# Another order of the weight tiles inside a group of a hybrid attention and pooling layer

## The chip, the cores and the metric

The kernel runs on one core of a Trainium2 chip. Its metric is the device time of one execution in microseconds. The engines are TensorE (PE, matrix products), VectorE (DVE), ScalarE (ACT), GpSimd (POOL) and SyncE (SP, which here only issues DMAs). Each works through its own list of instructions in order and waits for the others by semaphores.

## The reference

One layer takes 1024 frames of 2048 numbers, with 16 learned meta tokens ahead of them. Cut to what matters here:

```python
hn = _rmsnorm(h, norm_g)
pv, pg, q, k, v, ag = jnp.split(hn @ w_in, SPLITS, axis=-1)
# pooling: 4 channel groups, windows 2, 4, 8, 16
cg = jnp.cumsum(pv, axis=1)[..., group]
d = (cg - shifted_by_w(cg)) / cnt - pv[..., group]
pool_out = (d @ pool_w[group]) * pool_scale
# attention: 16 query heads, 2 key heads, window of two 64-frame chunks, meta tokens, a sink per head
attn_out = softmax_with_sink(q @ k.T / 8) @ v
h = h + concat([silu(pg) * pool_out, silu(ag) * attn_out]) @ w_out
```

## The kernel before, in words

The frames are worked on in two halves of 512. A half has 136 blocks of the input weights: 8 for keys and values, 32 for queries, and then four groups (g = 0 to 3) of 24 blocks. Four blocks in a row are one tile of 128 output channels, so a group has six tiles: two gates of attention (gates 0 and 1), the two tiles of pooling values, and two gates of pooling (gates 2 and 3). After both halves come 112 blocks of the output product.

To keep float32 accuracy on TensorE, each weight block is split into a high and a low part. SP loads a block into one of four raw buffers (line 400). ACT copies it to its high part `wh` (L616), VectorE subtracts for the low part `wl` (L964), and PE does three products for each of four slices, twelve matmuls to a block (L1435, L1436, L1442). ACT and VectorE split block s + 3 while PE works on block s. "Place s" of their lists means that split with all the work that the lists `todo` and `ahead` put beside it. ACT's split in place s waits until PE has finished block s - 1.

Beside the tiles each group runs the attention of four units of two heads (u = 0 to 3), written out by place. PE does the scores of a unit after blocks a and a + 1, its transposes after block a + 5 and its value products after block a + 7, where a is 2, 7, 11, 15 in group 0 and 0, 5, 10, 15 in groups 1 to 3. Between them lie, on VectorE, the sums of the scores (L1154), the row maximum (L1158, L1162) in place a + 2, and the normalising (L1168 to L1179) in place a + 4; on ACT the exponentials (L844, L847) in place a + 3. In place a + 6 ACT copies the transposed parts and VectorE takes their low parts (`pt`, `pm`), and in place a + 8 ACT (`o_low`) and VectorE (`o_out`, L1198 to L1206) take the unit's output. `qs` are the high and low parts of the queries for the next unit.

A gate's tile is read from its bank by VectorE (`gate_in`, L1212), ACT takes the tanh (L870) and VectorE closes it (`gate_out`, L1216). All four gates share one buffer for the tanh. Pooling values are copied out by ACT (`pv_out`, in front of the split of its place), in the first half from two banks, since 16 columns of earlier frames or meta tokens belong to them. POOL scales a tile (L578; in the first half after a small product, L573) and adds it up in g + 1 steps (L586), each of which doubles the window. Then VectorE subtracts (`pooled`, L1221), ACT and VectorE make the high and low parts of d (`d_high`, `d_low`), and at the end of the group PE multiplies d by `pool_w` (L1675 to L1677) and VectorE multiplies by gate and scale (`mix_out`, L1131). After each chain of sums POOL also issues two 1 MB DMAs that build sums of output weights (`weight_sums`). In the first half SP also stores finished tiles and loads frames of the next half (`spill`, `next_frames`) behind the loads of blocks 6 and 14.

The tiles share three PSUM banks R0 to R2. Before a tile PE waits until its bank has been read (`gate_bank_read`, `s_pve`). In the first half the second pooling tile starts on its first bank and waits for its second one, which the first pooling tile filled, in the middle of its first block (`second_free`).

Of the kernel before, what the change touches and what calls it, by code (L numbers as in the profile page):

```python
# [51 lines left out]
ROWT = HALF // P  # L52
UNITS = 4

FIRST_SPLITS = ({3: (1, 2), 7: (3, 4), 11: (5, 6), 15: (7,)},
# [35 lines left out]
def hymba_layer(nc, xcat, norm_g, w_in, w_out, pool_w, vecs, consts, out):  # L91
# [6 lines left out]
    with ctx:  # L98
# [130 lines left out]
        KB, VB = ((R[0], R[1]), (PM,)), ((R[2], O), (R[0],))  # L229
        PVB = (((R[2], R[0]), (R[1], R[2])), ((R[2],), (R[1],)))  # L230

# [139 lines left out]
        def product_done(eng, h, n):  # L371

            eng.wait_ge(s_blk, ONE + h * IN_BLKS + n + TILE_BLKS)
# [21 lines left out]
        def _(sp):  # L395
# [44 lines left out]
            for h in range(HALVES):  # L440
                h0 = h * IN_BLKS
                for n in range(RAW if h == 0 else 0, KV_BLKS):
                    if h and n == KV_BLKS - 1:
                        spill(GROUPS - 1)
                    load_block(h0 + n, n % RAW, w_in[TILE_BLKS * (n % 2) + n // 2, :, :])
                if h:
                    next_frames(GROUPS - 1)
                with sp.Fori(0, PAIRS) as j:
                    for b in range(TILE_BLKS):
                        n = KV_BLKS + j * TILE_BLKS + b  # L450
                        load_block(h0 + n, b % RAW, w_in[n, :, :])

                def group(g):
                    sp.wait_ge(s_pwl, ONE + h * GROUPS + g)
                    sp.dma_start(pw_raw.rearrange("p (a c) -> p a c", a=2),
                                 pool_w[g, :, :].rearrange("(a p) c -> p a c", p=P)).then_inc(s_pw, 16)
                    for b in range(G_BLKS):
                        n = KV_BLKS + Q_BLKS + g * G_BLKS + b
                        load_block(h0 + n, b % RAW, w_in[n, :, :])
                        if h == 0 and g and b == 6:  # L460
                            spill(g - 1)
                        if h == 0 and g and b == 14:
                            next_frames(g - 1)

                if h == 0:
                    for g in range(GROUPS):
                        group(g)
                else:
                    with sp.Fori(0, GROUPS) as g:
                        group(g)  # L470
# [143 lines left out]
        def _(act):  # L614
# [51 lines left out]
            for h in range(HALVES):  # L666
# [168 lines left out]
                def group(g):  # L835
# [36 lines left out]
                    def pv_out(jj):  # L872
                        product_done(act, h, n0 + 8 + 4 * jj)
                        act.wait_ge(s_dl, ONE + G * 2)
# [30 lines left out]
                    todo[4].append((gate_tanh, 0, R[0]))  # L905
                    todo[8].append((gate_tanh, 1, R[1]))
                    todo[16].append((d_high, 0))
                    todo[20].append((gate_tanh, 2, R[0]))
                    todo[21].append((d_high, 1))
                    todo[24].append((gate_tanh, 3, R[1]))  # L910
# [13 lines left out]
                    for s in range(G_BLKS + 1):  # L924
                        if s == 12:
                            pv_out(0)
                        elif s == 16:
                            pv_out(1)
# [33 lines left out]
        def _(dve):  # L962
# [27 lines left out]
            for h in range(HALVES):  # L990
# [145 lines left out]
                def group(g):  # L1136
# [73 lines left out]
                    def gate_in(n, bank):  # L1210
                        product_done(dve, h, n0 + (0, 4, 16, 20)[n])
                        nc.vector.tensor_tensor(gate[n], bank[:, :], rb[:, META:COLS], ALU.mult).then_inc(s_gv[n], 1)  # L1212
# [45 lines left out]
                    todo[5].append((gate_out, 0))  # L1258
                    todo[8].append((gate_in, 1, R[1]))
                    todo[9 if g else 14].append((gate_out, 1))  # L1260
                    todo[15].append((pooled, 0))
                    todo[18].append((d_low, 0))
                    todo[20].append((pooled, 1))
                    todo[22].append((d_low, 1))
                    todo[20].append((gate_in, 2, R[0]))
# [153 lines left out]
        def _(pe):  # L1419
# [89 lines left out]
            for h in range(HALVES):  # L1509
# [9 lines left out]
                def gate_bank_read(n, count):  # L1519
                    pe.wait_ge(s_gv[n], ONE + count)  # L1520
# [59 lines left out]
                def group(g, e, late):  # L1580
# [62 lines left out]
                    def events(s):  # L1643
                        for f, *a in when.get(s, ()):
# [9 lines left out]
                    gate_bank_read(3, G)  # L1654
                    tile(h, n0 + 4, (R[1],), own, events=events, slot0=4)
                    gate_bank_read(0, G + 1)
                    pe.wait_ge(s_pve, ONE + G * 2)
                    pe.wait_ge(s_me, ONE + G * 2)
                    tile(h, n0 + 8, PVB[h][0], pv_spans(h, g), events=events, slot0=8)
                    gate_bank_read(1, G + 1)  # L1660
                    tile(h, n0 + 12, PVB[h][1], pv_spans(h, g), events=events, slot0=12,
                         second_free=2 * G + 1 if h == 0 else 0)
                    pe.wait_ge(s_pve, ONE + G * 2 + 1)
                    tile(h, n0 + 16, (R[0],), own, events=events, slot0=16)
                    pe.wait_ge(s_pve, ONE + G * 2 + 2)
                    tile(h, n0 + 20, (R[1],), own, events=events, slot0=20)
# [119 lines left out]
```

## Time and profile before

| | |
|---|---|
| time, median of 3 runs | 1179.48 us (1178.87 to 1179.82) |
| the profiled execution | 1178.72 us, of which the span is 1176.6 us |
| busy, share of the span | PE 1166.1 us (99%), weight load 991.8 (84%), VectorE 889.7 (76%), ACT 616.1 (52%), POOL 115.5 (10%) |
| chain that ended last | PE 99% |
| costliest lines outside PE | L964 (low parts) 283.4 us, L616 (high parts) 240.8 us, L1084 (reciprocals) 53.6 us, L844 (exponentials) 51.2 us |
| POOL's sums | L586 50.3 us in 40 operations of 1257 ns, L578 20.9 us in 16 |
| DMA | 171.26 MB, mean 146 GB/s |

The span goes from the first to the last instruction that the profiler shows; the time also has what lies around it. "Busy" is the union of an engine's instructions, so that overlapping matmuls count once.

### The profile page before, as it was taken

The page shows a single profiled execution, that of the slowest core. Times are in us where ns is not written, and L with a number is a line of the kernel's source. Part 1 is how long each engine was busy: PE and PEld are TensorE (multiplying, and loading weights), DVE is VectorE, ACT ScalarE, POOL GpSimd, SP SyncE. Part 2 cuts the span into 40 slices and gives each one's busy share as a digit, 9 for nine tenths or more (in the row PEclk, how much of TensorE's full clock was granted, in tenths as well). Part 3 has the DMA queues.
Part 4 walks back from the last instruction along what each step waited for, and adds up shares of the span by engine and source line. Part 5 has one row for each costly group of instructions (what it writes and reads, how often), then busy time and mean ns, then how long its engine had stood idle before and what let it go on. Part 6 is the DMA issues. An engine that isn't in the chain of part 4 may idle for free.

```text
span 1176.6 us, 17280 instructions
## 1 busy us (share of the span) xinstructions
PE 1166.1 (99%) x5882; PEld 991.8 (84%) x5882; DVE 889.7 (76%) x1545; ACT 616.1 (52%) x1400; POOL 115.5 (10%) x133
## 2 busy tenths in 40 slices
PE   7999999999999999999999999999999999999998
PEld 7888898898898988888888888888888888888887
DVE  4678778787786885678788786987977977656676
ACT  5743366554665655643565655655544544444442
POOL 0000011020040220000011030220400000100001
PEclk9999999999999999999999999999999999999999
DMA  7354339455486333445357372392346544553443
GB/s 242 92 162 156 95 99 218 132 189 184 132 177 179 118 90 108 134 138 171 94 129 179 92 242 76 97 226 81 88 137 223 167 136 134 185 176 123 142 145 134
DMA packets 85486, 171.26 MB, mean 146 GB/s; under 512 B 8464, under 2 KB 11792, under 8 KB 85264
## 3 DMA queue, kind: packets, MB, share of 16 engines
q1 hardware_dynamic: 72000, 129.08, 35.3%
q0 software_dynamic: 13120, 40.90, 14.1%
q8 instruction: 44, 0.72, 0.3%
q14 instruction: 34, 0.28, 0.1%
q10 hardware_dynamic: 288, 0.28, 0.1%
HBM read 157.64 MB, written 46.14 MB: 173 GB/s over the span
## 4 chain that ended last, share of the span: by engine, by line
PE 99%; DMA 0%; DVE 0%; ACT 0%; issue 0%; SPq 0%; DVEq 0%; ACTq 0%
PE R L1435 18%; PE R L1436 18%; PE R L1442 18%; PE R L1725 3%; PE R L1723 3%; PE R L1724 3%; PE OP L1725 2%; PE S L1725 2%; PE OP L1723 2%; PE S L1723 2%; PE OP L1724 2%; PE S L1724 2%; PE S L1593 1%; PE OP L1617 1%; PE OP L1442 1%; PE OP L1435 1%
## 5 line engine op out<-in xcount | busy, mean ns | idle before, releaser
L964 DVE TENSOR_TENSOR wl<-raw,wh 128x512 fp32r<-128x512 f32 x384 | 283.4, 740 | 192.9 <-ACT wh L616 190.6
L616 ACT ACTIVATE wh<-raw 128x512 fp32r<-128x512 f32 x384 | 240.8, 629 | 351.0 <-PE OP L1725 165.9
L1435 PE MATMUL R<-act_h,wh 128*128 128x512 f32 (+5 forms) x1056 | 380.6, 365 | 0.0
L1436 PE MATMUL R<-act_l,wh 128*128 128x512 f32 (+5 forms) x1056 | 378.5, 364 | 0.0
L1442 PE MATMUL R<-act_h,wl 128*128 128x512 f32 (+5 forms) x1048 | 362.2, 365 | 0.0
L1436 PEld LDWEIGHTS R<-act_l,wh 128*128 128x128 f32 x1056 | 198.6, 188 | 28.6
L1435 PEld LDWEIGHTS R<-act_h,wh 128*128 128x128 f32 x1056 | 198.3, 188 | 28.7
L1442 PEld LDWEIGHTS R<-act_h,wl 128*128 128x128 f32 x1048 | 188.3, 188 | 32.1
L1725 PE MATMUL R<-wh,mix_l 128*128 128x512 f32 x168 | 65.4, 389 | 0.0
L1723 PE MATMUL R<-wh,mix_h 128*128 128x512 f32 x168 | 65.4, 389 | 0.0
L1724 PE MATMUL R<-wl,mix_h 128*128 128x512 f32 x168 | 65.4, 389 | 0.0
L870 ACT ACTIVATE row_buf<-scr 128x512 f32<-128x512 f32 x32 | 20.2, 632 | 79.5 <-DVE scr L1212 79.5
L1154 DVE TENSOR_REDUCE scr<-S 128x288 f32<-128x576 f32 x56 | 42.3, 756 | 25.3 <-PE S L1593 24.5
L1084 DVE RECIPROCAL scr<-scr 128x512 f32<-128x512 f32 x16 | 53.6, 3347 | 0.0
L844 ACT ACTIVATE scr<-scr,nmax 128x144 f32<-128x144 f32 x128 | 51.2, 403 | 3.4 <-DVE nmax L1162 3.3
L586 POOL TENSOR_TENSOR scr<-scr 128x513 f32<-128x513 f32 (+6 forms) x40 | 50.3, 1257 | 3.1
L578 POOL TENSOR_TENSOR scr<-scr,row_buf 128x512 f32<-128x512 f32 (+4 forms) x16 | 20.9, 1306 | 268.3 <-ACT scr L616 257.9
L1725 PE MATMUL OP<-wh,mix_l 128*128 128x512 f32 x112 | 43.6, 389 | 0.0
L1724 PE MATMUL OP<-wl,mix_h 128*128 128x512 f32 x112 | 43.6, 389 | 0.0
L1723 PE MATMUL S<-wh,mix_h 128*128 128x512 f32 x112 | 43.6, 389 | 0.0
L1724 PE MATMUL S<-wl,mix_h 128*128 128x512 f32 x112 | 43.6, 389 | 0.0
L1725 PE MATMUL S<-wh,mix_l 128*128 128x512 f32 x112 | 43.6, 389 | 0.0
(252 smaller groups left out, 1957.8 us busy)
## 6 DMA issues: line engine op xcount, KB each, us to landing
raw<-w_in_blocks SPq DMA_DIRECT2D x271, 256.0 KB, 2.7
wsum<-w_out_in POOLq DMA_DIRECT2D x24, 1024.0 KB, 12.1
raw<-wsum SPq DMA_DIRECT2D x64, 256.0 KB, 2.6
raw<-w_out_in SPq DMA_DIRECT2D x48, 256.0 KB, 3.3
c<-xcat SPq DMA_DIRECT2D x32, 256.0 KB, 3.5
out<-c POOLq DMA_DIRECT2D x28, 256.0 KB, 2.9
mixed<-xcat SPq DMA_DIRECT2D x10, 512.0 KB, 5.2
mx<-mixed SPq DMA_DIRECT2D x8, 512.0 KB, 3.5
```

The lines of the kernel that those rows point to most:

```text
L586: ins = pool.tensor_tensor(dst[:, lo:COLS], src[:, lo:COLS], src[:, lo - step:COLS - step], ALU.add)
L616: return nc.scalar.activation(dst, src, ACT.Copy)
L844: nc.scalar.activation(prob[:, c, :], prob[:, c, :], ACT.Exp, bias=nmax[:, c:c + 1], accum_out=den[:, c:c + 1]).then_inc(s_ex, 1)
L964: return nc.vector.tensor_tensor(dst, a, b, ALU.subtract)
L1084: nc.vector.reciprocal(q_rs[t % 2], q_rs[t % 2]).then_inc(s_qrs, 1)
L1154: nc.vector.tensor_reduce(to, both, AX.X, ALU.add).then_inc(s_sm, 1)
L1435: mm(o, wh[:, b, w], xh, start=(k == 0), stop=False)
L1436: mm(o, wh[:, b, w], xl, start=False, stop=False)
L1442: last = mm(o, wl[:, b, w], xh, start=False, stop=(k == KT - 1))
L1723: mm(banks[r], mh, wh[:, slot, :], start=(k == 0), stop=False)
L1724: mm(banks[r], mh, wl[:, slot, :], start=False, stop=False)
L1725: last = mm(banks[r], ml, wh[:, slot, :], start=False, stop=(k == HK - 1))
```

## The change

The blocks of a group come in another order: gate 0, the two pooling tiles, gate 1, gates 2 and 3. SP takes the addresses of the blocks from a table, the layout in memory stays as it was. ACT's copies of the pooling tiles, VectorE's subtraction and both parts of d are put four places sooner, so that POOL's sums follow four blocks sooner, and gate 1's read, tanh and closing product eight places later (the closing product from place 9, in group 0 from 14, to 17). The banks of the two pooling tiles and PE's waits for them are exchanged to match.

```diff
--- before.py
+++ after.py
@@ -51,6 +51,9 @@
 IN_BLKS = KV_BLKS + Q_BLKS + GROUPS * G_BLKS
 ROWT = HALF // P
 UNITS = 4
+
+GROUP_TILES = (0, 2, 3, 1, 4, 5)
+GATE_BLK = (0, 12, 16, 20)
 
 FIRST_SPLITS = ({3: (1, 2), 7: (3, 4), 11: (5, 6), 15: (7,)},
                 {3: (3,), 7: (4,), 11: (5, 6), 15: (7,)})
@@ -227,7 +230,7 @@
         OP = ctx.enter_context(nc.psum_tensor("OP", [P, 2, BLK], f32))
         O, PM = OP[:, 0, :], OP[:, 1, :]
         KB, VB = ((R[0], R[1]), (PM,)), ((R[2], O), (R[0],))
-        PVB = (((R[2], R[0]), (R[1], R[2])), ((R[2],), (R[1],)))
+        PVB = (((R[2], R[1]), (R[0], R[2])), ((R[2],), (R[0],)))
 
         OV = OP[:, :, :].rearrange("p b (c s n) -> p (b c) s n", c=2, s=2)
         QB = [S[:, 0, :]] + [(R[1][:, :], R[0][:, :], O)[t % 3] for t in range(PAIRS - 1)]
@@ -455,8 +458,9 @@
                     sp.dma_start(pw_raw.rearrange("p (a c) -> p a c", a=2),
                                  pool_w[g, :, :].rearrange("(a p) c -> p a c", p=P)).then_inc(s_pw, 16)
                     for b in range(G_BLKS):
-                        n = KV_BLKS + Q_BLKS + g * G_BLKS + b
-                        load_block(h0 + n, b % RAW, w_in[n, :, :])
+                        n = KV_BLKS + Q_BLKS + g * G_BLKS
+                        load_block(h0 + n + b, b % RAW,
+                                   w_in[n + GROUP_TILES[b // TILE_BLKS] * TILE_BLKS + b % TILE_BLKS, :, :])
                         if h == 0 and g and b == 6:
                             spill(g - 1)
                         if h == 0 and g and b == 14:
@@ -870,7 +874,7 @@
                         nc.scalar.activation(gate_t, gate[n], ACT.Tanh, scale=0.5).then_inc(s_ge[n], 1)
 
                     def pv_out(jj):
-                        product_done(act, h, n0 + 8 + 4 * jj)
+                        product_done(act, h, n0 + 4 + 4 * jj)
                         act.wait_ge(s_dl, ONE + G * 2)
                         for n, (bank, c) in enumerate(zip(PVB[h][jj], pv_spans(h, g))):
                             ins = copy(pv[jj][:, c], bank[:, 0:c.stop - c.start])
@@ -903,10 +907,10 @@
                         todo[22].append((qdiag, 0, g + 1))
                     todo[2].append((pw_high,))
                     todo[4].append((gate_tanh, 0, R[0]))
-                    todo[8].append((gate_tanh, 1, R[1]))
-                    todo[16].append((d_high, 0))
+                    todo[16].append((gate_tanh, 1, R[1]))
+                    todo[12].append((d_high, 0))
                     todo[20].append((gate_tanh, 2, R[0]))
-                    todo[21].append((d_high, 1))
+                    todo[17].append((d_high, 1))
                     todo[24].append((gate_tanh, 3, R[1]))
                     if isinstance(g, int) and g == 2:
                         todo[2].append((v_operand, 1))
@@ -922,9 +926,9 @@
                             for n, s in enumerate((21, 22, 24)):
                                 todo[s].append((mix_high, n))
                     for s in range(G_BLKS + 1):
-                        if s == 12:
+                        if s == 8:
                             pv_out(0)
-                        elif s == 16:
+                        elif s == 12:
                             pv_out(1)
                         if s == 1 and isinstance(g, int) and g == 0:
                             q_sqrt(PAIRS - 1)
@@ -1208,7 +1212,7 @@
                                                        ALU.mult, ALU.mult).then_inc(s_oe, 1)
 
                     def gate_in(n, bank):
-                        product_done(dve, h, n0 + (0, 4, 16, 20)[n])
+                        product_done(dve, h, n0 + GATE_BLK[n])
                         nc.vector.tensor_tensor(gate[n], bank[:, :], rb[:, META:COLS], ALU.mult).then_inc(s_gv[n], 1)
 
                     def gate_out(n):
@@ -1256,12 +1260,12 @@
                     todo[6].insert(0, (pw_low,))
                     todo[4].append((gate_in, 0, R[0]))
                     todo[5].append((gate_out, 0))
-                    todo[8].append((gate_in, 1, R[1]))
-                    todo[9 if g else 14].append((gate_out, 1))
-                    todo[15].append((pooled, 0))
-                    todo[18].append((d_low, 0))
-                    todo[20].append((pooled, 1))
-                    todo[22].append((d_low, 1))
+                    todo[16].append((gate_in, 1, R[1]))
+                    todo[17].append((gate_out, 1))
+                    todo[11].append((pooled, 0))
+                    todo[14].append((d_low, 0))
+                    todo[16].append((pooled, 1))
+                    todo[18].append((d_low, 1))
                     todo[20].append((gate_in, 2, R[0]))
                     todo[21].append((gate_out, 2))
                     todo[24].append((gate_in, 3, R[1]))
@@ -1652,17 +1656,17 @@
                     tile(h, n0, (R[0],), own, events=events, slot0=0)
                     pe.wait_ge(s_qn, h * PAIRS + 8)
                     gate_bank_read(3, G)
-                    tile(h, n0 + 4, (R[1],), own, events=events, slot0=4)
-                    gate_bank_read(0, G + 1)
                     pe.wait_ge(s_pve, ONE + G * 2)
                     pe.wait_ge(s_me, ONE + G * 2)
-                    tile(h, n0 + 8, PVB[h][0], pv_spans(h, g), events=events, slot0=8)
-                    gate_bank_read(1, G + 1)
-                    tile(h, n0 + 12, PVB[h][1], pv_spans(h, g), events=events, slot0=12,
+                    tile(h, n0 + 4, PVB[h][0], pv_spans(h, g), events=events, slot0=4)
+                    gate_bank_read(0, G + 1)
+                    tile(h, n0 + 8, PVB[h][1], pv_spans(h, g), events=events, slot0=8,
                          second_free=2 * G + 1 if h == 0 else 0)
                     pe.wait_ge(s_pve, ONE + G * 2 + 1)
+                    tile(h, n0 + 12, (R[1],), own, events=events, slot0=12)
+                    pe.wait_ge(s_pve, ONE + G * 2 + 2)
                     tile(h, n0 + 16, (R[0],), own, events=events, slot0=16)
-                    pe.wait_ge(s_pve, ONE + G * 2 + 2)
+                    gate_bank_read(1, G + 1)
                     tile(h, n0 + 20, (R[1],), own, events=events, slot0=20)
 
                     pe.wait_ge(s_dl, ONE + G * 2 + 2)
```

## Rows read from the trace of the kernel before

**Rows 1.** Waits, TensorE alone: total us, times, longest.

```profile
PE R L1453 <- DMA scr<-xcat: 5.7, 1, 5.7
```

**Rows 2.** Busy us (operations): PE, PEld, DVE, ACT, POOL; clock; DMA share; GB/s.

```profile
130.00:865.00 735.00, 734.83 (x3856) 630.27 (x3855) 580.05 (x1081) 417.88 (x1046) 95.65 (x92) 1.00 0.50 138
```

**Rows 3.** Timeline (start, length), PE, second half, group 1, end of block 10.

```profile
673.76 0.39 PE L1442 MATMUL R<-act_h,wl 128*128 128x512 f32 x1
674.00 0.60 PE L1605 MATMUL PT<-cst,scr 128*128 128x128 f32 x4
```

**Rows 4.** Timeline, VectorE, second half, group 1, places 8 and 9.

```profile
666.73 0.68 DVE L1198 TENSOR_TENSOR o_part<-OP,o_part 64x512 f32<-64x512 f32 x1
...
668.34 0.42 DVE L1206 SCALAR_TENSOR_TENSOR mixed<-scr 128x256 f32<-128x256 f32 x1
668.68 0.68 DVE L1212 TENSOR_TENSOR scr<-R,row_buf 128x512 f32<-128x512 f32 x1
670.59 0.69 DVE L964 TENSOR_TENSOR wl<-raw,wh 128x512 fp32r<-128x512 f32 x1 [1.22 <-ACT wh L616]
671.31 0.85 DVE L964 TENSOR_TENSOR qs<-mixed,qs 64x256 fp32r<-64x256 f32 x2
...
673.28 0.22 DVE L1179 TENSOR_TENSOR pnm<-scr,rden 128x64 f32<-128x64 f32 x1
```

**Rows 5.** Timeline, PE, second half, group 0, end of block 20.

```profile
629.37 0.62 PE L1605 MATMUL PT<-cst,scr 128*128 128x128 f32 x4
```

**Rows 6.** Timeline, VectorE, second half, group 0, places 16 to 19.

```profile
617.10 1.41 DVE L964 TENSOR_TENSOR wl<-raw,wh 128x512 fp32r<-128x512 f32 x1
...
620.58 1.18 DVE L964 TENSOR_TENSOR pm<-OP,pm 16x128 fp32r<-16x128 f32 x4
...
625.29 0.69 DVE L964 TENSOR_TENSOR wl<-raw,wh 128x512 fp32r<-128x512 f32 x1 [1.29 <-ACT wh L616]
...
629.06 0.22 DVE L1179 TENSOR_TENSOR pnm<-scr,rden 128x64 f32<-128x64 f32 x1
```

**Rows 7.** Timeline, ACT, second half, group 1, place 8.

```profile
665.35 0.63 ACT L616 ACTIVATE wh<-raw 128x512 fp32r<-128x512 f32 x1 [1.19 <-PE R L1442]
...
668.09 0.28 ACT L847 ACTIVATE esink<-nmax,vec 128x4 f32<-128x4 f32 x1
```

**Rows 8.** Operations with the tile raw: its loads, issue to landing.

```profile
DMA to landing us min/median/max: 2.4/2.7/10.2
```

**Rows 9.** Timeline, ACT, second half, group 3, place 12.

```profile
828.82 0.60 ACT L616 ACTIVATE scr<-R 128x512 f32<-128x512 f32 x1 [0.57 <-PE R L1442]
829.31 0.21 ACT L616 ACTIVATE scr<-pv_last 128x16 f32<-128x16 f32 x1
829.42 0.62 ACT L616 ACTIVATE wh<-raw 128x512 fp32r<-128x512 f32 x1
```

**Rows 10.** Timeline, POOL, second half, group 3, first chain.

```profile
829.60 1.29 POOL L578 TENSOR_TENSOR scr<-scr,row_buf 128x512 f32<-128x512 f32 x1 [56.60 <-ACT scr L616]
830.97 1.40 POOL L586 TENSOR_TENSOR scr<-scr 128x527 f32<-128x527 f32 x1
832.45 1.06 POOL L586 TENSOR_TENSOR scr<-scr 128x525 f32<-128x525 f32 x1
...
835.05 1.30 POOL L586 TENSOR_TENSOR scr<-scr 128x513 f32<-128x513 f32 x1
```

**Rows 11.** Timeline, VectorE, second half, group 3, beside that chain.

```profile
830.07 1.37 DVE L964 TENSOR_TENSOR wl<-raw,wh 128x512 fp32r<-128x512 f32 x1
...
835.59 1.05 DVE L1206 SCALAR_TENSOR_TENSOR mixed<-scr 128x256 f32<-128x256 f32 x1
```

**Rows 12.** Timeline, ACT, first half, group 3, place 8.

```profile
389.43 0.63 ACT L616 ACTIVATE wh<-raw 128x512 fp32r<-128x512 f32 x1 [1.16 <-PE R L1442]
```

**Rows 13.** Timeline, PE, first half, group 3, end of block 10.

```profile
398.63 0.60 PE L1605 MATMUL PT<-cst,scr 128*128 128x128 f32 x4
```

**Rows 14.** Timeline, ACT, second half, group 0, place 17.

```profile
618.19 1.13 ACT L616 ACTIVATE pm<-OP 16x128 fp32r<-16x128 f32 x4
```

## The prediction

> **What bounds the kernel now.** I read the waits of TensorE first, since an engine at 99% of the span is the bound unless it hides stops. Its longest wait by far is 5.7 us for the first load [rows 1], before anything that the change edits. The busy table of one long stretch, from shortly before the first group to the end of the last (130 to 865 us), has 734.83 us of PE in 735.00, at a granted clock of 1.00 [rows 2]. Inside the groups no idle time is left to win. A later, earlier or cheaper operation on another engine is worth nothing there; only a new stop of PE can move the time. So the question is how much slack stands in front of each thing that PE waits for, and I went from the waits to the timelines to measure it.
>
> Matmuls of one tile start 0.23 to 0.24 us apart [rows 3], 12 to a block, so a block takes 2.7 us at least and four blocks 11 us or more. In groups 1 to 3 PE's nearest appointment is the transposes of unit 1, which come at the end of block 10. In group 1 of the second half they start at 674.00 [rows 3], and the softmax pieces that they read were ready at 673.50 (673.28 + 0.22) [rows 4]: half a microsecond of slack. In group 0 the transposes of unit 3 (end of block 20) start at 629.37 [rows 5], their operand being ready at 629.28 (629.06 + 0.22) [rows 6]: 0.09 us, which is no slack but the time of the signal. Everything else that I measured (the low parts before the value products, the scores, the split weights) has more than a microsecond.
>
> **The change, part by part.** The same 24 blocks, matmuls, copies and loads are there before and after, so PE's sum of work is the same. A two-bank block (first half of the sequence) only stands at another place. SP issues the same 24 loads in another order from another address: 0. The banks: gate 1, which had R1 from block 4 to place 8, now has it from block 12 to place 16, and each tile that takes a bank still finds four blocks of 2.7 us between the read of it and its own start, as before. The second bank of pooling tile 1 is still given free by ACT's first copy at the start of the same block, and at that moment (place 8) ACT is idle and waiting for PE: its split there had waited 1.19 us for PE [rows 7], so the copy starts as promptly as it did at place 12. The wait for the previous group's mixing results moves from before block 8 to before block 4, but still has blocks 0 to 3, 11 us, in front of it. All that: 0. The wait for the last low parts of d before the mixing products is met four places sooner, where PE did not stop: 0.
>
> POOL's chain. It now runs in places 8 to 10 and 12 to 14 in place of 12 to 14 and 16 to 18. Its accumulating DMAs are issued four blocks sooner, one pair after the other at the same distance from each other. Between the last pair of the Q stage (issued at block 28) and the first group's (now behind block 48) some 20 blocks are left, over 50 us. The pair can now meet the loads of the next half's frames, which SP issues at place 8. Loads of a raw block land after 2.4 to 10.2 us [rows 8], and are issued about four blocks, 11 us, before ACT splits them, with three more blocks until PE wants them: 0.
>
> What costs is that ACT and VectorE get new work between the scores of unit 1 and its transposes. Laid onto the times of group 1 of the second half (block 7 ends just before 665.35):
>
> 1. ACT does the copies of pooling tile 0 first. Where they now stand, the split follows 0.60 us after the copy's start (829.42 against 828.82) [rows 9]. So the split at 665.35 [rows 7] comes at 665.95, is done at 666.58, and the exponentials, which ended at 668.37, end at 668.97.
> 2. In return gate 1's read (0.68 us) and its closing product (about as long) leave VectorE's places 8 and 9, and the tanh between them leaves ACT. They mattered: VectorE stood 1.22 us waiting for ACT's next split, which was behind that tanh [rows 4]. Without POOL's chain VectorE would take its low part of the weights at 669.7, and the softmax pieces would be ready near 672.6, sooner than now.
> 3. POOL's chain starts 0.78 us after ACT's copy (829.60 against 828.82) [rows 9, 10]: here at 666.1. And it holds VectorE up: a wl of 0.69 us takes 1.37 when it starts in a POOL operation, and ends 0.55 us after that operation (831.44 against 830.89) [rows 10, 11]. The POOL operation that comes next then ends 0.93 after the wl (832.37) [rows 10]. The 256-wide product of L1206, 0.42 us alone [rows 4], took 1.05 and ended 0.29 after POOL (836.64 against 836.35) [rows 10, 11]. Reductions and operations with a PSUM operand are not held up.
>
> The Trainium skill, "SBUF — State Buffer", section "SBUF: two separate sides", says the same of the cause: a VectorE operation with two SBUF inputs and a GpSimd operation that reads SBUF take one pair of ports by an exclusive lock, whoever starts first, for the whole instruction. The trace agrees with the waiting. By that rule a POOL operation that already waits would go before VectorE's next one, and the change would cost the 1.45 us of the alternating case below; by a VectorE that passes the ports on to itself it would cost nothing.
>
> Group 3 has five POOL operations. Op 1: 666.1 to 667.4. The wl of 666.58 ends at 667.95. Op 2 ends 668.9. The two kinds of o_out operations that read PSUM take 1.61 us (666.73 to 668.34) [rows 4], to 669.56. Op 3 (1.06 us [rows 10]) runs 668.95 to 670.0, so L1206 ends at 670.3. Now the trace of before has no row for what comes next: VectorE's next operations (wl, the two qs, the divisions) all have two SBUF inputs, and POOL waits for its turn. **If they alternate**, op 4 ends 671.2, wl 671.75, op 5 672.7, the first qs 672.95. From the end of the first qs (671.73) to the pieces' end (673.50) it is 1.77 [rows 4], so they are ready at 674.7, and with the 0.09 of the signal PE starts at 674.8 instead of 674.0: 0.8 us lost. **If VectorE keeps the ports**, wl ends 670.9, the pieces are ready at 673.1, and nothing is lost; POOL's chain ends some 2 us later, and has until place 11, which is after 677. In the first half's group 3 PE comes to the transposes 9.20 us after ACT's split of place 8 (398.63 against 389.43) [rows 12, 13] and not 8.65 (674.00 against 665.35) [rows 3, 7], and POOL has one small product more, 0.3 us by its place ahead of the chain: 0.8 - 0.55 + 0.3 = 0.55 lost. Group 2 has four POOL operations: the first qs starts at 671.8, the pieces are ready at 674.0, 0.1 lost in the second half and none in the first. Group 1, three operations: ready before 673.3, none. Sum if they alternate: 0.8 + 0.55 + 0.1 = 1.45 us; bound below: 0.
>
> Group 0, where there is no slack. From place 14 to 19 VectorE has five of the moved operations (low d 0, gate 1, pooled 1, closing product, low d 1) where it had three (closing product, pooled 0, low d 0): 2 x 0.68 = 1.36 us more before the normalising of unit 3. What covers it: POOL's second chain is gone from place 16, so that the wl at 617.10 takes 0.69 and not 1.41 [rows 6]; and in place 18 VectorE has 1.29 us in which it waits for ACT [rows 6], where two of the five (closing product and low d 1) fit. ACT is held by its tanh until gate 1 is read, near 617.8, so its small copies (618.19 to 619.32 [rows 14]) end 1.2 us later, at about 620.55, and VectorE takes the low parts from them at 620.6, when it does now (620.58) [rows 6]. The row maximum and all behind it stay in their place within 0.1 us. I take 0 to 0.1 for each half; bound above: 1.36 each, 2.7 us together, if no cover holds.
>
> **The sum.** The profiled run took 1178.72 us, 2.12 more than its span of 1176.6, and the median of the three runs 1179.48, 0.76 above it. 1178.72 + 1.45 = 1180.2, with group 0's 0 to 0.1 left at 0; against the median 1180.9. The bounds put together: 0 below, 1.45 + 2.7 = 4.15 above.
>
> **Rivals.** *POOL and VectorE do not alternate, or the loss is otherwise swallowed.* For it: the work taken from places 8 and 9 is larger than the work put there. Time: 1179.5. *VectorE falls behind in group 0.* For it: a slack of 0.09 us and five operations for three, with ACT held behind a tanh; against it, the two covers. With nothing covered, 1179.48 + 4.15 = 1183.6, slower; it decides from 0.9 us for each half on (with the 1.45, over 2.36). *DMAs collide*: POOL's megabyte sums beside the frames' loads. A raw load would have to land over 15 us after its issue to stop PE (seven blocks of 2.7, less the splits); the worst landed after 10.2 [rows 8]. Under 1 in 50. *Faster*: PE would have to have a wait in the groups that the new order removes. All that [rows 2] leaves is 0.17 us, and the time would be 1179.3, no change either.
>
> **Chances.** Alternating, 1180.9 or so: 0.40. Nothing lost, 1179.5: 0.36. Group 0 behind, by part or all of its 2.7, to 1183.6: 0.19; some of this stays under the bound. Something that I don't see, to either side: 0.05. I count a difference of over 0.2% (2.36 us) as change, about what a measurement of this kernel tells from none. Faster 0.04, same 0.78, slower 0.18. My value is that of the alternating case, 1180.9; the range goes from 1178.6 (the case of no loss, less the 0.9 us that runs of before differ by) to 1183.6. The likeliest case alone is 1180 to 1181.5.
>
> **What would show it.** In the trace after: no idle time of PE in blocks 4 to 11, and none at the second bank in block 8; the split of place 8 on ACT 0.6 us later; the wl of places 8 and 9 stretched by POOL and those of 16 and 17 not; a wait of PE for L1179 before the transposes of unit 1 in group 3, under a microsecond, none in group 1; the transposes of unit 3 in group 0 within 0.1 us of the end of block 20's matmuls. I am wrong if PE waits in group 0 for over half a microsecond, or in group 1 at all, or if the sum of PE's busy time changes by more than its waits.

## The result, and the profile after

The changed kernel takes 1181.88 us (median of 20 runs, 1180.71 to 1183.9), the kernel before 1179.8 us beside it (20 runs, 1178.87 to 1181.77). The ratio is 1.0017, with a 95% interval of 1.001 to 1.0024: slower by 2.1 us, and clear of noise, though the middle of the interval lies under the 0.2% that I had taken as a bound. I had forecast 1180.9, from three runs of the kernel before whose median was 1179.48; the twenty have 0.32 us more.

The waits of TensorE in the changed kernel (total us, times, longest; before, [rows 1] had the first of them as the longest, and the last two were there too):

```profile
PE R L1457 <- DMA scr<-xcat: 5.3, 1, 5.3
PE PT L1609 <- DVE pnm L1183: 1.6, 2, 1.0
PE R L1499 <- DVE act_l L980: 1.0, 1, 1.0
PE OP L1499 <- DVE act_l L980: 0.2, 1, 0.2
```

One line is new: twice the transposes wait for the softmax pieces of VectorE. (Lines after the diff are four higher, so L1609 is what L1605 was, and L968, L1183, L1210 and L590 are L964, L1179, L1206 and L586.) The busy table of the stretch with the groups, which in [rows 2] left PE 0.17 us idle, now leaves 1.80:

```profile
130.00:867.00 737.00, 735.20 (x3855) 629.82 (x3854) 579.75 (x1082) 420.53 (x1046) 97.17 (x92) 1.00 0.50 138
```

The larger of the two waits is in group 3 of the second half. On ACT, whose split of place 8 would have come at 817.35 or so, the copies of pooling tile 0 are first, and the split comes 0.74 us after their start:

```profile
817.30 0.60 ACT L620 ACTIVATE scr<-R 128x512 f32<-128x512 f32 x1 [1.10 <-PE R L1446]
817.91 0.22 ACT L620 ACTIVATE scr<-pv_last 128x16 f32<-128x16 f32 x1
818.04 0.62 ACT L620 ACTIVATE wh<-raw 128x512 fp32r<-128x512 f32 x1
```

POOL's chain beside it (operations 1 to 3; 4 and 5 as one row, 822.19 to 825.02):

```profile
818.21 1.30 POOL L582 TENSOR_TENSOR scr<-scr,row_buf 128x512 f32<-128x512 f32 x1 [55.11 <-ACT scr L620]
819.58 1.39 POOL L590 TENSOR_TENSOR scr<-scr 128x527 f32<-128x527 f32 x1
821.05 1.06 POOL L590 TENSOR_TENSOR scr<-scr 128x525 f32<-128x525 f32 x1
...
822.19 2.83 POOL L590 TENSOR_TENSOR scr<-scr 128x521 f32<-128x521 f32 x2
```

VectorE in the same stretch:

```profile
818.69 1.36 DVE L968 TENSOR_TENSOR wl<-raw,wh 128x512 fp32r<-128x512 f32 x1 [0.63 <-ACT wh L620]
819.97 0.67 DVE L1202 TENSOR_TENSOR o_part<-OP,o_part 64x512 f32<-64x512 f32 x1
820.68 0.87 DVE L1206 TENSOR_TENSOR scr<-OP,o_part 64x256 f32<-64x256 f32 x2
821.58 0.82 DVE L1210 SCALAR_TENSOR_TENSOR mixed<-scr 128x256 f32<-128x256 f32 x1
822.32 1.54 DVE L968 TENSOR_TENSOR wl<-raw,wh 128x512 fp32r<-128x512 f32 x1
823.89 1.85 DVE L968 TENSOR_TENSOR qs<-mixed,qs 64x256 fp32r<-64x256 f32 x2
...
826.86 0.22 DVE L1183 TENSOR_TENSOR pnm<-scr,rden 128x64 f32<-128x64 f32 x1
```

As long as POOL's chain runs, each operation with two operands in SBUF is stretched: the low part of the weights twice (0.69 alone), L1210 from 0.42 to 0.82, the pair of `qs` from 0.85 [rows 4] to 1.85 (all of it in the first of the two). L1202, which reads the PSUM bank OP, runs inside POOL's second operation and takes its usual 0.67. The second wl starts at 822.32, 0.13 us after POOL's fourth operation has been issued, and ends at 823.86. PE then stands still for 0.96 us:

```profile
825.78 0.39 PE L1446 MATMUL R<-act_h,wl 128*128 128x512 f32 x1
827.13 0.66 PE L1609 MATMUL PT<-cst,scr 128*128 128x128 f32 x4 [0.96 <-DVE pnm L1183]
```

Without the wait the transposes would have started 0.23 to 0.24 us after the matmul, as in [rows 3], at 826.02. So 1.11 us are lost. Group by group, from the end of a group's start block to the end of its last one (worked out from the matmuls that close the blocks), against the kernel before:

| us over before | group 0 | group 1 | group 2 | group 3 |
|---|---|---|---|---|
| first half | +0.24 | -0.12 | -0.07 | +0.79 |
| second half | +0.19 | -0.02 | +0.09 | +1.13 |

The eight sum to 2.23. With the start of the run, 0.09 us shorter, and rounding they are the 2.13 us by which the last matmul comes later, and the span grew by 2.1 (1176.6 to 1178.7). Behind the groups nothing moved: the output stage has the same length to 0.01 us.

### The profile page after: what moved, and what is told of

Same layout as the page of the kernel before. It is cut to its first block, busy times and chain, and to the rows that moved or that the text cites. A ratio compares the mean times of both kernels' runs of the same rounds, so it can differ in the third digit from the quotient of the medians.

```text
span 1178.7 us, 17282 instructions
## 1 busy us (share of the span) xinstructions
PE 1167.0 (99%) x5882; PEld 992.1 (84%) x5882; DVE 889.2 (75%) x1545; ACT 618.9 (53%) x1400; POOL 117.0 (10%) x133
## 4 chain that ended last, share of the span: by engine, by line
PE 97%; DVE 2%; DMA 0%; issue 0%; ACT 0%; SPq 0%; ACTq 0%; DVEq 0%
PE R L1439 18%; PE R L1440 18%; PE R L1446 18%; PE R L1727 3%; PE R L1729 3%; PE R L1728 3%; PE S L1727 2%; PE OP L1727 2%; PE OP L1729 2%; PE S L1729 2%; PE OP L1728 2%; PE S L1728 2%; PE S L1597 1%; PE PT L1609 1%; PE OP L1446 1%; PE OP L1440 1%
## 5 line engine op out<-in xcount | busy, mean ns | idle before, releaser
L968 DVE TENSOR_TENSOR wl<-raw,wh 128x512 fp32r<-128x512 f32 x384 | 281.1, 734 | 192.1 <-ACT wh L620 191.2
L590 POOL TENSOR_TENSOR scr<-scr 128x513 f32<-128x513 f32 (+6 forms) x40 | 51.7, 1293 | 3.1
L1727 PE MATMUL OP<-wh,mix_h 128*128 128x512 f32 x112 | 43.6, 389 | 0.0
```

Of the source, the lines that this page charges most:

```text
L590: ins = pool.tensor_tensor(dst[:, lo:COLS], src[:, lo:COLS], src[:, lo - step:COLS - step], ALU.add)
L968: return nc.vector.tensor_tensor(dst, a, b, ALU.subtract)
L1727: mm(banks[r], mh, wh[:, slot, :], start=(k == 0), stop=False)
```

## The experiments

Each was timed beside the kernel before on the same chip. The groups' sums are against the profiled kernel before, as in the table above; each is one execution, but they leave out the stages ahead of the groups, whose end moved by up to 1.0 us from run to run.

| run | median us | before | ratio (95%) | groups, first half | groups, second half |
|---|---|---|---|---|---|
| changed kernel | 1181.88 | 1179.8 | 1.0017 (1.001 to 1.0024) | 0.24, -0.12, -0.07, 0.79 | 0.19, -0.02, 0.09, 1.13 |
| sums late | 1182.86 | 1179.77 | 1.0025 (1.0015 to 1.0035) | 2.29, -0.12, -0.07, -0.09 | 1.95, -0.02, 0.00, -0.01 |
| short chain | 1179.13 | 1179.77 | 0.9993 (0.9984 to 1.0002) | 0.22, -0.12, -0.07, -0.09 | 0.25, 0.00, 0.09, -0.01 |
| five operations | 1184.73 | 1179.77 | 1.0041 (1.0028 to 1.0055) | 0.59, 0.51, 0.54, 0.75 | 0.37, 0.81, 0.87, 1.16 |
| queries behind | 1180.8 | 1179.77 | 1.0012 (1.0003 to 1.0021) | 0.20, -0.14, -0.07, 0.25 | 0.25, 0.00, 0.00, 0.73 |
| tanh later | 1181.17 | 1179.87 | 1.0007 (0.9998 to 1.0016) | 0.02, -0.12, -0.07, 0.76 | 0.03, 0.00, 0.07, 1.14 |
| copy behind | 1185.85 | 1179.87 | 1.0049 (1.0036 to 1.0063) | 0.23, -0.12, -0.07, 0.78 | 0.25, 0.81, 1.55, 4.16 |
| both repairs | 1180.92 | 1179.87 | 1.0009 (1.0 to 1.0018) | 0.02, -0.12, -0.07, 0.25 | 0.03, 0.00, 0.00, 0.72 |
| queries ahead | 1179.88 | 1179.73 | 0.9999 (0.999 to 1.0008) | -0.01, -0.12, -0.07, -0.06 | 0.04, 0.00, 0.00, 0.74 |

My theory after the result: POOL and VectorE take turns at operations with two SBUF operands, and in group 3 the chain is long enough to hold up VectorE until PE waits. The rival: ACT's copy, now ahead of the exponentials, delays them by 0.6 us, and VectorE only follows.

### Sums late: the new order with POOL at its old places

```diff
                         pool.wait_ge(s_pve, ONE + (h * GROUPS + g) * 2 + jj + 1)
+                        pool.wait_ge(s_blk, ONE + h * IN_BLKS + KV_BLKS + Q_BLKS + g * G_BLKS + 12 + 4 * jj)
...
-                    todo[12].append((d_high, 0))
+                    todo[16].append((d_high, 0))
-                    todo[17].append((d_high, 1))
+                    todo[21].append((d_high, 1))
...
-                    todo[11].append((pooled, 0))
-                    todo[14].append((d_low, 0))
-                    todo[16].append((pooled, 1))
-                    todo[18].append((d_low, 1))
+                    todo[15].append((pooled, 0))
+                    todo[18].append((d_low, 0))
+                    todo[20].append((pooled, 1))
+                    todo[22].append((d_low, 1))
```

> The new order of blocks and of gate 1, but POOL's sums start four blocks later, where they stood before, and the subtraction and both parts of d go back to their places (15 to 22). Theory (ports shared by POOL and VectorE make the waits): PE's wait before the transposes of unit 1 in group 3 (0.96 and 0.62 us) and the 0.1 us of group 2 are gone. In group 0 the cover that I counted on is gone too: VectorE has gate 1's two operations beside POOL's chain in places 16 and 17, so that the wait before the transposes of unit 3, 0.2 us now, should grow to between 0.7 and 1.5 us in each half. Time within 1 us of the changed kernel. Rival (ACT's copy ahead of the exponentials makes them): the waits of group 3 stay at 0.6 us or more.

The waits of groups 2 and 3 are gone (group 3 is at -0.01 and -0.09), with ACT's copy still ahead of the exponentials. The rival as the whole cause is out. The time is 0.98 us over the changed kernel, just inside what I had written. What I did not see is a part of the other side: group 0 grew by 2.29 and 1.95 us. The wait before the transposes, 1.1 us, is in the range of 0.7 to 1.5, but there were two waits, not one. The first waits of TensorE in that kernel:

```profile
PE PT L1610 <- DVE pnm L1184: 2.1, 2, 1.1
PE OP L1622 <- ACT pm L621: 0.8, 1, 0.8
PE OP L1622 <- issue: 0.4, 1, 0.4
```

ACT's tanh of gate 1 waits for VectorE, which waits for POOL; behind the tanh on ACT stand unit 2's small copies, and PE's value products of unit 2 wait for those, a wait that I had not priced (in the second half ACT stands for 4.32 us before that tanh). Each half loses about 2 us, which my rival on group 0 had bounded at 1.36, and moving POOL's chain forward avoids it: the new order of blocks needs the sooner sums.

### Short chain: three POOL operations in group 3

```diff
-                        for lev in range(g + 1):
+                        last = min(g, 1) if g == 3 else g
+                        for lev in range(last + 1):
...
-                            if lev < g:
+                            if lev < last:
```

> The changed kernel, with POOL's chain in group 3 cut from five operations to three (it leaves out the last two doublings, so group 3's pooling is that of a window of 4). Theory (ports): group 3 behaves as group 1, PE's wait before the transposes of unit 1 there is gone in both halves, time 1.8 to 2.1 us under the changed kernel. Rival (ACT's copy): waits of 0.6 us or more stay, time within 0.7 us of the changed kernel.

Group 3 is as long as before to 0.1 us in both halves, and no wait of PE for the pieces is left in the trace. ACT's copy stands where it stood. The median fell by more than I had written (2.75 us, 1181.88 to 1179.13, not timed side by side, against 1.8 to 2.1) and more than the groups account for (2.0).

### Five operations in every group

```diff
                         src = pv[jj]
+                        for _ in range(GROUPS - 1 - g):
+                            if chained:
+                                pool.wait_ge(s_add, chained)
+                            pool.tensor_tensor(psum_w[1][:, first + 1:COLS], src[:, first + 1:COLS],
+                                               src[:, first:COLS - 1], ALU.add).then_inc(s_add, 1)
+                            chained += 1
```

> The changed kernel, with additional POOL additions (their results are overwritten) so that each group's chain has five operations, as group 3's. Theory (ports): groups 1 and 2 now lose what group 3 loses, 1.0 to 1.2 us each in the second half and 0.6 to 0.9 each in the first, so 3.2 to 4.2 us over the changed kernel, less the 0.1 that group 2 loses now; group 0 adds 0 to 1 us, since its unit 2 meets a longer second chain with 1.1 us of slack. Rival (ACT's copy): no change, within 0.7 us of the changed kernel.

The loss follows the number of POOL operations:

```profile
PE PT L1615 <- DVE pnm L1189: 4.1, 7, 1.0
```

Groups 1 and 2 go from about 0 to 0.5 in the first half and to 0.81 and 0.87 in the second, group 0 adds 0.35 and 0.18. Over the changed kernel the eight groups have 3.37 us more (5.60 against 2.23), inside what I had written, with each second-half group some 0.15 under its part; by the medians, not timed side by side, it is 2.85 (1184.73 against 1181.88), under it. Without additional ACT work the waits came into groups that had none.

### Queries behind the normalising

```diff
-                        if u < UNITS - 1 and at[u + 1] - 1 == at[u] + 4:
+                        behind = g > 0 and u == 1
+                        if not behind and u < UNITS - 1 and at[u + 1] - 1 == at[u] + 4:
                             todo[at[u] + 4].append((qdiag, u + 1, g))
...
                             todo[at[u] + 4].append((normalise, u))
+                        if behind:
+                            todo[at[u] + 4].append((qdiag, u + 1, g))
```

> The changed kernel, with VectorE's two low parts of the queries for unit 2 (groups 1 to 3) behind unit 1's normalising in place 9 and not ahead of it. Theory (VectorE's queue, held by POOL, sets the pieces): the first operation of the normalising meets POOL's fifth operation instead, but 0.85 us of queue are gone, so the wait in group 3 falls from 0.96 to 0.0 to 0.3 us in the second half and to 0 in the first, time 1.5 to 2.0 us under the changed kernel. The scores of unit 2, which wait for the moved parts, have over 3 us of slack and lose at most 1.5. Rival (the exponentials, late by ACT's copy, set the pieces): nothing changes, since the normalising waits for them.

The wait before the transposes shrank as expected, from 1.1 us to 0.2, but a new one took part of its place. PE in group 3 of the second half:

```profile
825.74 0.39 PE L1449 MATMUL R<-act_h,wl 128*128 128x512 f32 x1
826.19 0.66 PE L1612 MATMUL PT<-cst,scr 128*128 128x128 f32 x4
...
827.16 0.53 PE L1600 MATMUL S<-band,qs 128*128 128x288 f32 x2 [0.20 <-DVE qs L968]
```

and VectorE:

```profile
823.73 1.27 DVE L1172 TENSOR_TENSOR dtot<-den,esink 128x4 f32<-128x4 f32 x1
...
826.17 0.86 DVE L968 TENSOR_TENSOR qs<-mixed,qs 64x256 fp32r<-64x256 f32 x2
```

The scores of unit 2 come in the same pause of PE as unit 1's transposes, and the queries' low parts, which had over 3 us of slack, now have none. The group saved 0.4 us in the second half and 0.54 in the first, not 1.1 and 0.9, and the median is 1.1 us under the changed kernel, where I had written 1.5 to 2.0. The first of the rows on VectorE is instructive by itself: a sum over four columns, 0.16 us alone, takes 1.27: it has two SBUF operands, and POOL's fifth operation, which ends 0.02 us before it, is in front of it. (A rival by which ACT's exponentials set the pieces is out here too: they would have been as late.)

### Group 0's tanh later

```diff
-                    todo[16].append((gate_tanh, 1, R[1]))
+                    if g:
+                        todo[16].append((gate_tanh, 1, R[1]))
...
                     todo[17].append((d_high, 1))
+                    if not g:
+                        todo[17].append((gate_tanh, 1, R[1]))
```

> The changed kernel, with gate 1's tanh in group 0 behind unit 2's small copies and the high part of d on ACT (place 17) and not ahead of them (place 16). Theory (in group 0 ACT is held behind the tanh until VectorE has read gate 1, and the row maximum follows late): the small copies start some 1.5 us earlier, and the 0.2 us before the transposes of unit 3 are gone in each half; at most 0.4 us in all, too little for the times, so the blocks and the wait decide. Rival (VectorE has too many operations in places 16 to 18): the 0.2 us stay.

Group 0's 0.24 and 0.19 fall to 0.02 and 0.03. The cause was ACT held behind the tanh, not the number of VectorE's operations.

### ACT's copy behind the exponentials, second half only

```diff
-                        if s == 8:
+                        if s == 8 and h == 0:
                             pv_out(0)
...
                         for f, *a in todo[s]:
                             f(*a)
+                        if s == 8 and h:
+                            pv_out(0)
```

> The changed kernel; in the second half alone ACT's copy of pooling tile 0 stands behind the exponentials of place 8 and not ahead of the split, so that the exponentials come 0.6 us sooner and POOL's first chain starts some 3 us later. Theory (ports): the chain now lies on VectorE's queries' low parts and on the normalising itself, which all have two operands in SBUF, so PE waits before the transposes of unit 1 also in groups 1 and 2 of the second half, and in group 3 no less than 0.8 us; time 0.5 to 3 us over the changed kernel. Rival (ACT's copy ahead of the exponentials): the wait of group 3 in the second half falls by 0.6 us, and groups 1 and 2 have none.

This was the sharpest test, since theory and rival say opposite signs, and it went the way of the ports: in the profiled execution groups 1 to 3 of the second half lost 0.81, 1.55 and 4.16 us, though their exponentials came sooner. The first half, which was not edited, is as in the changed kernel. VectorE in group 3, second half:

```profile
825.13 1.36 DVE L970 TENSOR_TENSOR wl<-raw,wh 128x512 fp32r<-128x512 f32 x1 [0.89 <-ACT wh L620]
826.52 2.38 DVE L970 TENSOR_TENSOR qs<-mixed,qs 64x256 fp32r<-64x256 f32 x2
828.93 0.90 DVE L1174 TENSOR_TENSOR dtot<-den,esink 128x4 f32<-128x4 f32 x1
829.87 0.18 DVE L1176 RECIPROCAL rden<-dtot 128x4 f32<-128x4 f32 x1
830.08 1.38 DVE L1181 TENSOR_TENSOR scr<-scr,rden 128x256 f32<-128x256 f32 x1
```

and POOL (operations 3 and 4 as one row):

```profile
824.66 1.28 POOL L582 TENSOR_TENSOR scr<-scr,row_buf 128x512 f32<-128x512 f32 x1 [58.16 <-ACT scr L620]
826.02 1.39 POOL L590 TENSOR_TENSOR scr<-scr 128x527 f32<-128x527 f32 x1
827.49 2.32 POOL L590 TENSOR_TENSOR scr<-scr 128x525 f32<-128x525 f32 x2
829.89 1.28 POOL L590 TENSOR_TENSOR scr<-scr 128x513 f32<-128x513 f32 x1
```

Five POOL operations, five stretched ones on VectorE (the wl, both `qs`, dtot and the first product behind the reciprocal), in strict turn; only the reciprocal, with one operand, takes its usual 0.18. By the medians the run is 4.0 us over the changed kernel, more than the 3 that I had given as the most, and the profiled execution, one of the longest of the five, has 5.4 more in its groups. A second reason for that, in this execution, is told in the last section.

### Both repairs, and the queries ahead

"Both repairs" is the two edits above (queries behind, tanh later) in one kernel.

> The changed kernel with both repairs: the queries' low parts behind unit 1's normalising, and in group 0 gate 1's tanh behind the small copies. Theory: PE's waits in the groups fall under 0.3 us in sum, and the time comes to within 0.5 us of the kernel before, on either side: PE was busy throughout in it, so nothing beyond that can be had. Rival (the new order costs PE something besides its waits): 0.7 us or more over the kernel before with no wait in the trace.

The rest of group 3 stays (0.72 and 0.25), group 0 is repaired; the sum of the groups is 0.83 us over before, so over the 0.3 that I had written. The median is 1.05 us over before, outside the 0.5 too. There is no loss outside the waits of group 3, which speaks against this run's rival. The last kernel has the tanh later and puts the queries' low parts ahead instead, into the 0.6 us in which VectorE waits for ACT's split:

```diff
-                        if u < UNITS - 1 and at[u + 1] - 1 == at[u] + 4:
+                        if g and u == 1:
+                            ahead[8].append((qdiag, u + 1, g))
+                        elif u < UNITS - 1 and at[u + 1] - 1 == at[u] + 4:
                             todo[at[u] + 4].append((qdiag, u + 1, g))
```

> The changed kernel with gate 1's tanh in group 0 behind the small copies, and in groups 1 to 3 the two low parts of the queries for unit 2 at the head of VectorE's place 8, ahead of the low part of the weights, where VectorE waits for ACT's copy and split anyway. Theory (in group 3 it is the operations with two SBUF operands behind POOL's third operation that are each held up): the queue behind POOL's fourth operation is then the low part of the weights and the normalising alone, so the wait in group 3 falls from 0.96 and 0.62 us to under 0.4 in the second half and 0 in the first, with no new wait before the scores of unit 2; the blocks of the groups sum to within 0.4 us of the kernel before, the time to 0.7 us. Rival (each operation moved out only makes the one behind it wait as long): 0.6 us or more stay in group 3 of the second half.

1179.88 us against 1179.73, ratio 0.9999 (0.999 to 1.0008): by the medians the loss of the change is undone. The first half is shorter than before in all four groups, by 0.26 us in all, and its wait in group 3 is gone. Group 3 of the second half keeps one wait of 0.5 us and 0.74 of length, over the 0.4 that I had written, so the eight groups sum to 0.52 over before and not to 0.4 at most. The rival, which wanted 0.6 or more there, fits that one group and not the first half:

```profile
817.64 1.86 DVE L971 TENSOR_TENSOR qs<-mixed,qs 64x256 fp32r<-64x256 f32 x2
819.54 1.44 DVE L971 TENSOR_TENSOR wl<-raw,wh 128x512 fp32r<-128x512 f32 x1
...
823.24 1.80 DVE L971 TENSOR_TENSOR wl<-raw,wh 128x512 fp32r<-128x512 f32 x1
```

The second of the two `qs` began 0.28 us behind POOL's first operation (818.08 against 817.80) and took 1.43 us, and the low part of place 9, the last row, had POOL's fifth operation (823.11 to 824.49) in front of it. No kernel beat the one before by more than its interval.

## Why the prediction was right

**PE is the bound and only a new stop can move the time.** Right: the loss is made of waits of PE, and with most of them removed the median is that of before. Only the reading of [rows 2] was too strict: the busy time hides short stops between matmuls, so that the new order could win 0.28 us in the first half (below), where the table left 0.17 in all.

**Where it would stop.** Right in groups 1 to 3: transposes of unit 1 in group 3 (both halves), 0.1 us in group 2 of the second half, nothing in group 1. The signs that I named for them came too: the split of place 8 later by 0.7 us, the wl of places 8 and 9 stretched, those of 16 and 17 in group 0 at 0.68. The chance of "no loss" because VectorE keeps the ports (0.36) fell: the two alternate. Against POOL's fourth operation, which was issued at 822.19 while L1210 held the ports until 822.40 (821.58 + 0.82), the wl at 822.32 had to wait. In the kernel with the copy behind, it is so five times in a row. The Trainium skill, "SBUF — State Buffer", section "SBUF: two separate sides", has whoever starts first hold the pair for its whole instruction; these rows agree, and show what follows from it for two queues that both always have a next operation: turn by turn.

**Its size.** This is what was off, though the time stayed in the range; it passed the 1180 to 1181.5 that I had given for the likeliest case alone. Of the 0.95 us between 1180.93 and 1181.88, 0.32 are the median of the kernel before, and the rest are the terms. The term for group 3 of the second half was 0.8 and measured 1.1. By its own steps: first qs done at 7.7 us after block 7 by my sum, at 8.0 in the trace (825.32 against 817.27, the end of the block). POOL's fourth operation ended where I had it (5.95 by the sum, 6.0 in the trace). The fifth and last one ended 1.17 us after the wl (825.02 against 823.86) and not 0.93. That last one was 0.24 us longer than the rule I had taken from one of the middle ones; my rows had a last operation [rows 10] that met no such wl. The remaining 0.1 was there from the start of the chain: POOL's first operation came 0.94 us after the end of the block (818.21 against 817.27), where my sum has 0.85, and each operation behind it is set by that. ACT's split did come 0.74 us after the copy and not 0.60, but that moved nothing, as the wl had to wait for POOL's first operation anyhow. The term for the first half was 0.55 and measured 0.88 (0.79 in the changed kernel against -0.09 with the short chain); its fifth operation too ended 1.17 us after the wl.

**Group 0.** I took 0 to 0.1 in each half, and it was 0.24 and 0.19; the sign that I named, transposes within 0.1 us of the end of block 20's matmuls, did not come. The covers held to 0.2 us. Of the chain, ACT's small copies were late by that much: VectorE's low parts waited for them,

```profile
621.53 1.19 DVE L968 TENSOR_TENSOR pm<-OP,pm 16x128 fp32r<-16x128 f32 x4 [0.34 <-ACT pm L620]
```

6.71 us after block 15, where it had been 6.50 (620.58 in [rows 6], block 15 having ended at 614.08), and the pieces came as much later. The run with the tanh later shows that this was all. The kernel with the sums late shows what the cover by POOL's absence was worth: 2.05 and 1.76 us over the changed kernel, more than my bound of 1.36, since I had left out the value products; the wait before the transposes alone grew by 1.0.

**Sum.** 1.45 + 0 to 0.1 in each half predicted; 1.14 + 0.88 + 0.09 + 0.24 + 0.19 = 2.54 measured, less 0.28 that groups 1 to 3 of the first half gained and 0.03 in groups 1 and 3 of the second, so 2.23. The gain is about 0.1 us a group, and at least in group 1 it lies where the second pooling tile changes to its second bank: before, one matmul there starts 0.22 us after the one ahead of it (249.44 to 249.66) and its like 0.12, and in the changed kernel all of that block do. I had put that at 0. By my own bound of 2.36 us the result is "same", which had 0.78, but only by 0.3 us. So the mechanism and the places were right, and the value came out 0.95 us low: the two terms of group 3 were too small by 0.3 each and group 0 by 0.4 in all, the 0.3 won in the first half made up for a part, and the base was 0.3 low. That the range held is also due to its upper end, which a case of its own, group 0 behind, sets.

**What hides nothing.** DMAs: raw loads still land after 2.7 us, 10.7 at worst (10.2 in [rows 8]), and PE waits for none. The banks and the mixing wait: no idle time there.

## What to carry to other kernels

When one engine is busy all the time, list the appointments that it has with the others, and measure the slack of each from the trace before moving anything: here they were 0.1 and 0.5 us, and every loss of the changed kernel was found there. Two of the experiments lost at the next ones, which had looked roomy (the value products of unit 2, the scores of unit 2). Moving a queue of POOL work is moving a toll on VectorE: each POOL operation can stretch one VectorE operation with two SBUF operands, however small (by 0.4 to 1.1 us in the rows above, beside POOL operations of 1.1 to 1.6), so put the chain beside PSUM reads, reductions or idle time, and never beside a short chain of small operations that something waits for. And an operation that is put out of one critical piece of a queue must be checked against its own reader.

## What the runs showed of the hardware

A stop of TensorE can cost more than its length. In the kernel with the copy behind, PE stood still for 2.36 us before the transposes, and the busy table by stretches shows the granted clock then at 0.51, the lower of its two levels (1.2 of 2.4 GHz), until about 835.3:

```profile
829.00:831.90 2.90, 0.63 (x3) 0.19 (x1) 2.83 (x6) 0.63 (x1) 2.10 (x2) 1.00 0.00 0
831.90:834.00 2.10, 2.01 (x8) 1.94 (x9) 0.80 (x3) 0.65 (x2) 0.00 (x0) 0.51 0.12 24
834.00:836.00 2.00, 2.00 (x7) 1.58 (x6) 1.99 (x4) 1.54 (x5) 0.00 (x0) 0.66 0.30 106
836.00:838.00 2.00, 2.00 (x11) 1.66 (x10) 1.90 (x6) 0.62 (x3) 0.00 (x0) 1.00 0.45 131
```

Its matmuls started 0.43 us apart and not 0.23:

```profile
833.60 0.63 PE L1441 MATMUL R<-act_h,wh 128*128 128x512 f32 x1
834.02 0.63 PE L1442 MATMUL R<-act_l,wh 128*128 128x512 f32 x1
```

Of the 4.16 us that the group lost, 2.5 are the wait (829.24 + 0.23 to 831.99). The other 1.6 fit the slow clock: half speed from 831.9 to 835.3 costs 1.7. After the wait of 1.37 us in group 2 of the same execution (transposes at 753.93), and after that of 0.96 us in the changed kernel, the clock stayed at 1.00. So the longest of the three stops was charged twice, and the two shorter ones once. This is one execution, the only one of the run that left a trace: of the five, two have a span of 1185.2 us and three of 1182.4 to 1182.6. That the clock did not fall in those three would fit, but is not shown.
